# Gate and up products of an expert layer: two feed-forward tiles per accumulation group

## The chip, the cores and the metric

The kernel runs on one core of one Trainium2 chip. The metric is the device time of one execution in microseconds. Three executions of the kernel before gave 3181.3, 3182.09 and 3187.0 us, median 3182.09 us. One further execution was taken with the hardware profiler; every row below comes from it.

## What is computed

The program is one inference step of a two-layer backbone over 640 tokens (128 context, 512 latent) of width 1024. Layer 0 has a dense SwiGLU, layer 1 has eight SwiGLU experts of which each token takes two. Only the expert mixer is touched by the change:

```python
def swiglu(h, wg, wu, wd):
    return (jax.nn.silu(h @ wg) * (h @ wu)) @ wd       # 1024 -> 1408 -> 1024 for an expert

def moe_swiglu(h, router_w, router_b, wg, wu, wd):
    ...
    logits = (t @ router_w + router_b).astype(jnp.float32)
    top_v, top_i = lax.top_k(logits, TOP_K)             # 2 of 8
    w = jax.nn.softmax(top_v, axis=-1)
    gates = jnp.sum(jax.nn.one_hot(top_i, N_EXPERTS, dtype=jnp.float32) * w[..., None], axis=1).astype(t.dtype)
    y = jnp.zeros_like(t)
    for e in range(N_EXPERTS):
        y = y + gates[:, e:e + 1] * swiglu(t, wg[e], wu[e], wd[e])
    return y.reshape(B, L, D)
```

The reference computes it in float32. The kernel computes, of each expert, only the rows that chose it, and gets close to float32 with the rounded type fp32r: each operand is split into a high part (rounded to fp32r) and a low part (the operand minus its high part), and each product is the sum of three: high by high, high by low, low by high.

## The kernel before: the expert stage

**Items.** After routing, the rows of each expert lie in blocks of 128. There are `ITEMS` = 17 blocks, each with one expert's weights. An item needs 17 loads of weights (`ITEM_LOADS`): 11 of gate and up (`GU_LOADS` = `UF` = 11, the number of 128-wide tiles in 1408), and 6 of down (`DN_LOADS`), the last of which is half as long. A full load is 128 partitions by 2048 floats, 1 MB. A gate/up load holds, for one feed-forward tile f, all 8 blocks of the contraction (`KD` = 8), each with 128 gate columns and 128 up columns. q counts loads over all items, p within one item, i counts items.

**Slots.** A load lands in one of 8 slots (`M_SLOT`, `M_SLOTS`); its high part goes to one of 4 buffers (`M_HIGH`, `M_HI`); the low part overwrites the slot. SP's queue issues the even loads (L721), GpSimd's queue the odd ones (L2228); load q waits until TensorE has begun load q-7 (`m_used`, raised by a load's first matmul). SP's queue also carries an item's rows in (L726) and its results out (L730).

**TensorE** (L1259 to L1308), for each load of gate and up: wait for the low part of the load (`v_mlo`) and, at L1283, 24 matmuls (8 blocks by 3 products) of 256 moving columns into half of bank h % 2, h counting tiles over all items. Stationary are the rows, moving are the weights. After each tile but the first come the transposes of the tile before it (`turn_hidden`, L1267, one 128x128 transpose). After tile f = 8 (`M_TURN`) come the 8 transposes of the next item's rows (`turn_rows`, L1259). Then follow the down loads (L1305), 12 matmuls of 512 columns each; the transpose of the item's last tile is behind the first down load. Down load c reads the turned hidden tiles 2c and 2c+1.

**ScalarE**, at step p of an item: the high part of load q+3 (`moe_high`, L1581; it waits for the landing and for TensorE to have begun load q); at p = 0 the copies of the last item's results (`move_out`, L1596); silu of tile p's gate half (L1618, waits for TensorE, `s_mgu`); the high part of turned tile p-1 (L1589).

**VectorE**, at step p: the product silu by up of tile p (L1736, waits for silu); the low part of turned tile p-1 (L1740, waits for L1589); then the low part of load q+2 (`moe_low`, L1659, waits for its high part). All engines work strictly in the order of their programs, so the low part of load q+2 stands behind the product of tile p. During down loads there is no tile; the low part of the last turned tile is at L1748, that of the next item's rows at L1727.

Of the kernel before, what the change touches and what calls it, by code (L numbers as in the profile page):

```python
# [26 lines left out]
ALU = mybir.AluOpType  # L27
ACT = mybir.ActivationFunctionType
# [5 lines left out]
P = 128  # L34
D = 1024
KD = D // P
# [24 lines left out]
ALPHA = (2 * DEPTH) ** 0.25  # L61
LN_EPS, RMS_EPS = 1e-5, 1e-6
NEG = -1e30
# [19 lines left out]
RING_W = 2 * KD * P  # L83
# [99 lines left out]
def build(nc, x_in, cond_in, ada_bias_in, const_in, par_in, ln_in, ada_in, feat_in, tokm_in, out_in,  # L183
          unit_in, down_in, moe_gu_in, moe_down_in, zero_in, ctx_na_k, ctx_na_v, ctx_df_k, ctx_df_v, state_in, table_in,
          y_prompt, y_sample, new_na_k, new_na_v, new_df_k, new_df_v, new_state):
    with ExitStack() as ctx:
# [28 lines left out]
        def bank(b, lo=0, hi=BANK):  # L215
            return psum[:, b * BANK + lo:b * BANK + hi]
# [6 lines left out]
        ident, upper, lower, ones, blocks = (keep[:, i * P:(i + 1) * P] for i in range(5))  # L223
# [59 lines left out]
        def changing4(ap, d, m):  # L283
# [48 lines left out]
        HG = [m_hg[:, i * P:(i + 1) * P] for i in range(4)]  # L332

        HB = R12[:, (M_HI + M_SLOTS - RING) * RING_W:][:, 0:TILES * D].rearrange("p (t d) -> p t d", t=TILES)

# [62 lines left out]
        s_mtr = sem("moe_hidden_turned")  # L398
# [5 lines left out]
        a_msg = sem("act_moe_silu")  # L404
# [6 lines left out]
        v_mh = sem("vec_moe_hidden")  # L411
# [156 lines left out]

        def m_item(q):
            return q // ITEM_LOADS, q % ITEM_LOADS  # L570

        ALL_M = ITEMS * ITEM_LOADS

# [180 lines left out]
        def _(pe):  # L754
# [507 lines left out]
            def turn_hidden(i, f):  # L1262
                h = UF * i + f
                pe.wait_ge(v_mh, h + 1)
                if h >= 2:
                    pe.wait_ge(v_mhl, h - 1)
                pe.transpose(bank(2 + h % 2, 0, P), HG[h % 4], ident).then_inc(s_mtr, 1)  # L1267

            pe.wait_ge(a_hb, 2 * TILES)
            turn_rows(0)  # L1270
            for i in range(ITEMS):
                for f in range(UF):
                    h, q = UF * i + f, m_load(i, f)
                    pe.wait_ge(v_mlo, q + 1)
                    if f == 0:
                        pe.wait_ge(v_mxl, i + 1)
                    if h >= 2:
                        pe.wait_ge(v_mh, h - 1)
                    hi, lo = (r32(w).rearrange("p (k c) -> p k c", k=KD) for w in (M_HIGH[q % M_HI], M_SLOT[q % M_SLOTS]))
                    for k in range(KD):  # L1280
                        cols = slice(k * P, (k + 1) * P)
                        for m, (x, w) in enumerate(((XT_HI, hi), (XT_HI, lo), (XT_LO, hi))):
                            mm = pe.matmul(bank(h % 2, 0, 2 * P), r32(x[:, cols]), w[:, k, :],  # L1283
                                           start=(k == 0 and m == 0), stop=(k == KD - 1 and m == 2))
                            if q and k == 0 and m == 0:
                                mm.then_inc(m_used, 1)
                    mm.then_inc(s_mgu, 1)
                    if f:
                        turn_hidden(i, f - 1)
                    if f == M_TURN and i + 1 < ITEMS:  # L1290
                        turn_rows(i + 1)
                for c in range(DN_LOADS):
                    p = GU_LOADS + c
                    q = m_load(i, p)
                    pe.wait_ge(v_mlo, q + 1)
                    if c == 0 and i:
                        pe.wait_ge(a_mo, 2 * i)
                    hi, lo = (r32(w) for w in (M_HIGH[q % M_HI], M_SLOT[q % M_SLOTS]))
                    for j in range(m_words(p) // D):
                        f = 2 * c + j  # L1300
                        pe.wait_ge(v_mhl, UF * i + f + 1)
                        for g in range(2):
                            at = slice(j * D + g * BANK, j * D + (g + 1) * BANK)
                            for m, (x, w) in enumerate(((GT_HI, hi), (GT_HI, lo), (GT_LO, hi))):
                                mm = pe.matmul(bank(4 + g), r32(x[:, f, :]), w[:, at],  # L1305
                                               start=(f == 0 and m == 0), stop=(f == UF - 1 and m == 2))
                                if j == 0 and g == 0 and m == 0:
                                    mm.then_inc(m_used, 1)  # L1308
                            if f == UF - 1:
                                mm.then_inc(s_mdn, 1)  # L1310
                    if c == 0:
                        turn_hidden(i, UF - 1)

        @block.scalar
        def _(act):
# [271 lines left out]
            def hidden_turned_high(h):  # L1587
                act.wait_ge(s_mtr, h + 1)
                act.copy(r32(GT_HI[:, h % UF, :]), bank(2 + h % 2, 0, P)).then_inc(a_mhh, 1)  # L1589

            def move_out(i):
                if i >= 2:
# [13 lines left out]
            for i in range(ITEMS):  # L1606
                for p in range(ITEM_LOADS):
                    q = m_load(i, p)
                    if q + M_AHEAD < ALL_M:
                        moe_high(q + M_AHEAD)  # L1610
                    if p == 0 and i:
                        move_out(i - 1)
                    if p < UF:
                        h = UF * i + p
                        act.wait_ge(s_mgu, h + 1)
                        if h >= 4:
                            act.wait_ge(s_mtr, h - 3)
                        act.activation(HG[h % 4], bank(h % 2, 0, P), ACT.Silu).then_inc(a_msg, 1)  # L1618
                    if 1 <= p <= UF:
                        hidden_turned_high(UF * i + p - 1)  # L1620
# [22 lines left out]
        def _(v):  # L1643
# [79 lines left out]
            def moe_items():  # L1723

                def rows_low(i):
                    v.wait_ge(a_mxh, i + 1)
                    v.tensor_tensor(r32(XT_LO), psum[:, 6 * BANK:8 * BANK], high(XT_HI), ALU.subtract).then_inc(v_mxl, 1)  # L1727

                rows_low(0)
                for i in range(ITEMS):  # L1730
                    for p in range(ITEM_LOADS):
                        q = m_load(i, p)
                        if p < UF:
                            h = UF * i + p
                            v.wait_ge(a_msg, h + 1)
                            v.tensor_tensor(HG[h % 4], HG[h % 4], bank(h % 2, P, 2 * P), ALU.mult).then_inc(v_mh, 1)  # L1736
                        if 1 <= p < UF:
                            h = UF * i + p - 1
                            v.wait_ge(a_mhh, h + 1)
                            v.tensor_tensor(r32(GT_LO[:, h % UF, :]), bank(2 + h % 2, 0, P), high(GT_HI[:, h % UF, :]),  # L1740
                                            ALU.subtract).then_inc(v_mhl, 1)
                        n = q + 2
                        if n < ALL_M:
                            moe_low(n)
                        if p == UF:
                            h = UF * i + p - 1
                            v.wait_ge(a_mhh, h + 1)
                            v.tensor_tensor(r32(GT_LO[:, h % UF, :]), bank(2 + h % 2, 0, P), high(GT_HI[:, h % UF, :]),  # L1748
                                            ALU.subtract).then_inc(v_mhl, 1)
                        if p == UF + 2 and i + 1 < ITEMS:  # L1750
                            rows_low(i + 1)

# [570 lines left out]
def lay_out(x_prompt, x_sample, cache_na_k, cache_na_v, cache_df_k, cache_df_v, state_dn, c, c_ctx, ada_w, ada_b, w_in,  # L2323
# [53 lines left out]
    def expert_tiles(w):  # L2377
        return w[0].reshape(EXPERTS, KD, P, UF, 1, P).transpose(0, 3, 2, 1, 4, 5)

    a["moe_gu"] = np.concatenate([expert_tiles(moe_w_gate), expert_tiles(moe_w_up)], 4).reshape(EXPERTS, UF, P, KD * 2 * P)  # L2380
# [34 lines left out]
```

## Time and profile before

| | |
|---|---|
| median of three executions | 3182.09 us |
| span of the profiled execution, first to last instruction | 3180.0 us |
| TensorE busy | 2834.8 us, 89% |
| VectorE busy | 1780.5 us, 56% |
| ScalarE busy | 1319.6 us, 41% |
| L1283, gate and up, weights' high part moving | 3728 matmuls, 571.2 us |
| L1283, gate and up, weights' low part moving | 760 matmuls, 215.2 us |
| L1305, down, by its larger group | 940 matmuls, 252.0 us |
| L1283 in the chain that ended last | 15% of the span |
| L1305 in the chain that ended last | 8% of the span |

How to read it: an engine's busy time is the time in which one of its instructions was running. Matmuls overlap, each starting while the one before it drains, so that the mean duration of one (287 ns at L1283) is longer than the distance from one start to the next. That distance is read from the starts in the timeline. The granted TensorE clock stands as a share of full speed: 1.00 is 2.4 GHz, 0.50 is 1.2 GHz. It is 1.00 in the expert stage from the end of its first loads on. The first matmul of the stage starts at 2259.9 us and the last one at 3121.2 us; behind it lie the gathering of the rows and the closing norm.

### The profile page before, as it was taken

How to read it: one execution, taken by the hardware profiler on the slowest of the kernel's cores; microseconds unless marked ns; L12 is line 12 of the kernel's file. 1: busy time of each engine (PE TensorE's matmuls, PEld its weight loads, DVE VectorE, ACT ScalarE, POOL GpSimd, SP SyncE). 2: the span in 40 equal slices, each digit the busy share in tenths (PEclk: the TensorE clock that was granted, in tenths of full speed). 3: DMA queues.
4: the chain of work that ended last, by engine and by line, in shares of the span. 5: the costliest groups of instructions: out<-in, count | busy, mean ns of one | idle time of the engine just before them, and what ended most of it. 6: DMA issues, size and time to landing. Idle time of an engine off the chain costs nothing.

```text
span 3180.0 us, 51506 instructions
## 1 busy us (share of the span) xinstructions
PE 2834.8 (89%) x21524; PEld 2516.3 (79%) x21524; DVE 1780.5 (56%) x2706; ACT 1319.6 (41%) x1934; POOL 341.3 (11%) x335
## 2 busy tenths in 40 slices
PE   6998897997799999979988979978699999999992
PEld 5996776666799899769977756667699989899992
DVE  2244445666722222352534456676588888888886
ACT  2123222445222122131342224442477777777773
POOL 0002213000200000100012130011100000000002
PEclk9998997899999999979988978999899999999996
DMA  5233221000112221232122110003699999999993
GB/s 211 80 132 131 82 82 41 19 1 1 54 67 73 80 80 64 89 138 76 54 97 107 56 47 13 1 1 134 233 380 353 375 350 364 365 359 376 354 366 122
DMA packets 76517, 477.43 MB, mean 150 GB/s; under 512 B 10224, under 2 KB 13808, under 8 KB 26864
## 3 DMA queue, kind: packets, MB, share of 16 engines
q1 hardware_dynamic: 52672, 316.84, 26.6%
q0 software_dynamic: 23616, 157.30, 13.1%
q8 instruction: 173, 2.83, 0.4%
q14 instruction: 56, 0.46, 0.0%
HBM read 455.49 MB, written 27.53 MB: 152 GB/s over the span
## 4 chain that ended last, share of the span: by engine, by line
PE 76%; DVE 10%; ACT 5%; issue 4%; DMA 3%; POOL 1%; DVEq 0%; SPq 0%; ACTq 0%
PE psum L1283 15%; PE psum L1182 10%; PE psum L832 8%; PE psum L1305 8%; PE psum L1212 4%; PE psum L1143 4%; PE psum L858 3%; PE psum L1090 3%; DMA ring<-in_ada 2%; PE psum L956 2%; PE psum L1048 2%; PE psum L966 2%; ACT stage_rounded L1581 2%; PE psum L979 2%; PE psum L771 1%
## 5 line engine op out<-in xcount | busy, mean ns | idle before, releaser
L1283 PE MATMUL psum<-stage_rounded 128*128 128x256 f32 x3728 | 571.2, 287 | 11.1 <-DVE stage_rounded L1659 4.3
L1283 PEld LDWEIGHTS psum<-stage_rounded 128*128 128x128 f32 x3728 | 512.4, 191 | 28.3 <-DVE ring_rounded L1659 12.0
L1659 DVE TENSOR_TENSOR ring_rounded<-ring,stage_rounded 128x2048 fp32r<-128x2048 f32 (+1 forms) x145 | 319.4, 2217 | 2.4 <-ACT stage_rounded L1581 2.4
L1659 DVE TENSOR_TENSOR stage_rounded<-stage,stage_rounded 128x2048 fp32r<-128x2048 f32 (+1 forms) x144 | 318.1, 2224 | 0.0
L1581 ACT CAST stage_rounded<-ring 128x2048 fp32r<-128x2048 f32 (+1 forms) x145 | 269.4, 1864 | 44.8 <-PE psum L1305 28.7
L1581 ACT CAST stage_rounded<-stage 128x2048 fp32r<-128x2048 f32 (+1 forms) x144 | 268.7, 1870 | 44.2 <-PE psum L1305 28.4
L1305 PE MATMUL psum<-stage_rounded 128*128 128x512 f32 x940 | 252.0, 394 | 0.1
L1476 ACT ACTIVATE stage<-psum,arena 128x640 f32<-128x640 f32 (+1 forms) x180 | 126.4, 706 | 231.0 <-DVE arena L1984 231.0
L1283 PE MATMUL psum<-ring_rounded,stage_rounded 128*128 128x256 f32 x760 | 215.2, 283 | 0.0
L1305 PEld LDWEIGHTS psum<-stage_rounded 128*128 128x128 f32 x940 | 175.1, 188 | 43.0 <-DVE stage_rounded L1659 3.9
L1090 PEld LDWEIGHTS psum<-stage 128*128 128x128 f32 x1008 | 134.0, 203 | 68.2 <-issue 35.4
L1090 PE MATMUL psum<-stage 128*128 128x128 f32 x1008 | 153.1, 299 | 30.4 <-ACT stage L1483 16.9
L1182 PE MATMUL psum<-stage_rounded 128*128 128x320 f32 x704 | 161.8, 311 | 12.0 <-POOL ring_rounded L2309 12.0
L1551 ACT CAST stage_rounded<-ring 128x2048 fp32r<-128x2048 f32 (+2 forms) x38 | 64.0, 1685 | 239.8 <-PE psum L1182 130.9
L1984 DVE TENSOR_REDUCE arena<-psum 128x1 f32<-128x640 f32 (+1 forms) x180 | 123.1, 713 | 72.0 <-PE psum L1051 36.4
L1182 PE MATMUL psum<-input_rounded,stage_rounded 128*128 128x320 f32 x704 | 161.4, 310 | 0.0
L1182 PE MATMUL psum<-stage_rounded,ring_rounded 128*128 128x320 f32 x704 | 161.1, 310 | 0.0
L1283 PEld LDWEIGHTS psum<-ring_rounded,stage_rounded 128*128 128x128 f32 x760 | 145.8, 192 | 0.3
L1452 ACT COPY stage<-psum 128x512 f32<-128x512 f32 x100 | 58.5, 585 | 211.0 <-PE psum L966 211.0
L2146 DVE TENSOR_TENSOR stage<-stage,psum 128x640 f32<-128x640 f32 x22 | 18.1, 822 | 216.4 <-PE psum L1182 216.4
L2126 DVE TENSOR_TENSOR ring_rounded<-ring,stage_rounded 128x2048 fp32r<-128x2048 f32 (+2 forms) x36 | 71.9, 1996 | 115.7 <-ACT stage_rounded L1551 115.7
L1212 PE MATMUL psum<-stage_rounded 128*128 128x512 f32 x440 | 135.9, 389 | 0.0
(318 smaller groups left out, 5990.6 us busy)
## 6 DMA issues: line engine op xcount, KB each, us to landing
ring<-in_ada SPq DMA_DIRECT2D x48, 1024.0 KB, 5.0
ring<-in_moe_gu SPq DMA_DIRECT2D x48, 1024.0 KB, 7.0
ring<-in_moe_gu POOLq DMA_DIRECT2D x47, 1024.0 KB, 7.3
stage<-in_moe_gu SPq DMA_DIRECT2D x46, 1024.0 KB, 7.8
stage<-in_moe_gu POOLq DMA_DIRECT2D x46, 1024.0 KB, 7.9
ring<-in_unit SPq DMA_DIRECT2D x22, 1024.0 KB, 4.8
stage<-in_moe_down SPq DMA_DIRECT2D x22, 1024.0 KB, 7.6
stage<-in_moe_down POOLq DMA_DIRECT2D x22, 1024.0 KB, 7.8
```

Source lines behind the costliest of these rows:

```text
L832: mm = pe.matmul(bank(b + g, 0, HALF), w[:, i % 2, k, :], r32(x[:, k, g * HALF:(g + 1) * HALF]), start=(k == 0 and m == 0), stop=(k == KD ...
L858: mm = pe.matmul(bank(b, 0, 256 if c < TOKM_LOADS else P), r32(x[:, k, t * P:(t + 1) * P]), wk, start=(k == 0 and m == 0), stop=(k == KD - ...
L1090: mm = pe.matmul(bank(7, 256, 256 + P), probT[j % 2][:, s * P:(s + 1) * P], VT[:, s, v_at:v_at + P], start=(s == 0), stop=(s == n - 1))
L1143: mm = pe.matmul(bank(n % 4, 0, 256), r32(x[:, k, t * P:(t + 1) * P]), w[:, k, :], start=(k == 0 and m == 0), stop=(k == KD - 1 and m == 2))
L1182: mm = pe.matmul(bank(b + 2 * i + g, 0, HALF), w[:, i, k, :], r32(x[:, k, g * HALF:(g + 1) * HALF]), start=(k == 0 and n == 0), stop=(k == ...
L1212: mm = pe.matmul(bank(b), r32(x[:, f, cols]), w[:, j, :], start=(f == 0 and m == 0), stop=(f == UF - 1 and m == 2))
L1283: mm = pe.matmul(bank(h % 2, 0, 2 * P), r32(x[:, cols]), w[:, k, :], start=(k == 0 and m == 0), stop=(k == KD - 1 and m == 2))
L1305: mm = pe.matmul(bank(4 + g), r32(x[:, f, :]), w[:, at], start=(f == 0 and m == 0), stop=(f == UF - 1 and m == 2))
L1476: act.activation(dst, src, ACT.Exp, bias=nb[:, s:s + 1], accum_out=sm[:, s:s + 1]).then_inc(a_exp, 1)
L1581: act.copy(r32(M_HIGH[q % M_HI][:, 0:n]), M_SLOT[q % M_SLOTS][:, 0:n]).then_inc(a_mhi, 1)
L1659: v.tensor_tensor(r32(w), w, high(M_HIGH[q % M_HI][:, 0:n]), ALU.subtract).then_inc(v_mlo, 1)
L1984: v.tensor_reduce(nb[:, s:s + 1], src, AX.XY if t else AX.X, ALU.max, negate=True).then_inc(v_nb, 1)
```

## The change

Two feed-forward tiles share one accumulation group, and so one PSUM bank in its full width. Of the 11 tiles, 10 form five wide groups and the last stays alone (`GROUPS` = 6; `m_group(p)` gives a load's group and whether it is the group's last load, `m_width(g)` its width, 256 or 128 hidden columns).

- A wide group's weights are 2 MB as before, in two loads; but each now holds half of the contraction (4 blocks) for both tiles, 256 gate and 256 up columns, where it held all 8 blocks for one tile. The host lays the weights out so. Size, number, slots and order of the loads stay.
- A load of a wide group has 12 matmuls of 512 columns (4 blocks by 3 products), where it had 24 of 256. The group ends with its second load. The eleventh load is as before.
- silu, the product, and the high and low parts of the turned tiles are done once per group, 256 columns wide, at the step of the group's last load; in between they are absent. The transposes come in pairs behind the next group; those of the last group stay behind the first down load. The transposes of the next item's rows come after group 4 (load 9), where they came after load 8.
- There are two hidden buffers of 256 columns for four of 128. silu of group h waits for the transposes of group h-2.
- VectorE's low part of load q+2 stays at step p, as does ScalarE's high part of load q+3. So the low part of a group's first load is at a step without a product, and that of a group's second load stands behind the product and the low part of turned hidden tiles.

```diff
-M_TURN = UF - 3
+GROUPS = (UF + 1) // 2
+M_TURN = GROUPS - 2
@@ TensorE
-                pe.transpose(bank(2 + h % 2, 0, P), HG[h % 4], ident).then_inc(s_mtr, 1)
+                for j in range(m_width(g) // P):
+                    mm = pe.transpose(bank(2 + h % 2, j * P, (j + 1) * P), HG[h % 2][:, j * P:(j + 1) * P], ident)
+                mm.then_inc(s_mtr, 1)
...
-                for f in range(UF):
+                for p in range(GU_LOADS):
+                    (g, last), q = m_group(p), m_load(i, p)
+                    h, wide = GROUPS * i + g, 2 * m_width(g)
                     pe.wait_ge(v_mlo, q + 1)
...
-                    for k in range(KD):
+                    for j in range(n):
+                        k = first + j
                         cols = slice(k * P, (k + 1) * P)
                         for m, (x, w) in enumerate(((XT_HI, hi), (XT_HI, lo), (XT_LO, hi))):
-                            mm = pe.matmul(bank(h % 2, 0, 2 * P), r32(x[:, cols]), w[:, k, :],
+                            mm = pe.matmul(bank(h % 2, 0, wide), r32(x[:, cols]), w[:, j, :],
                                            start=(k == 0 and m == 0), stop=(k == KD - 1 and m == 2))
...
+                    if not last:
+                        continue
                     mm.then_inc(s_mgu, 1)
-                    if f:
-                        turn_hidden(i, f - 1)
-                    if f == M_TURN and i + 1 < ITEMS:
+                    if g:
+                        turn_hidden(i, g - 1)
+                    if g == M_TURN and i + 1 < ITEMS:
                         turn_rows(i + 1)
@@ ScalarE
-                    if p < UF:
-                        h = UF * i + p
+                    if p < UF and last:
+                        h, w = GROUPS * i + g, m_width(g)
                         act.wait_ge(s_mgu, h + 1)
-                        if h >= 4:
-                            act.wait_ge(s_mtr, h - 3)
-                        act.activation(HG[h % 4], bank(h % 2, 0, P), ACT.Silu).then_inc(a_msg, 1)
+                        if h >= 2:
+                            act.wait_ge(s_mtr, h - 1)
+                        act.activation(HG[h % 2][:, 0:w], bank(h % 2, 0, w), ACT.Silu).then_inc(a_msg, 1)
+                        if g:
+                            hidden_turned_high(i, g - 1)
@@ VectorE
-                        if p < UF:
-                            h = UF * i + p
+                        if p < UF and last:
                             v.wait_ge(a_msg, h + 1)
-                            v.tensor_tensor(HG[h % 4], HG[h % 4], bank(h % 2, P, 2 * P), ALU.mult).then_inc(v_mh, 1)
+                            v.tensor_tensor(HG[h % 2][:, 0:w], HG[h % 2][:, 0:w], bank(h % 2, w, 2 * w), ALU.mult).then_inc(v_mh, 1)
+                            if g:
+                                hidden_turned_low(i, g - 1)
                         n = q + 2
                         if n < ALL_M:
                             moe_low(n)
```

## Rows read from the trace of the kernel before

**Rows 1.** Busy time by window: us; PE, PEld, DVE, ACT, POOL, clock, DMA.
```profile
2400.00:2500.00 100.00, 98.92 (x694) 91.25 (x693) 84.18 (x81) 74.14 (x84) 8.97 (x17) 1.00 0.95 365
```

**Rows 2.** Chain of waits, 2440 to 2600 us: start us, us, what.
```profile
2469.87 3.13 PE psum L1283 x24
...
2473.11 2.87 PE psum L1283 x24
...
2491.78 0.87 PE psum L1259 x8
...
2520.53 3.13 PE psum L1283 x24
```

**Rows 3.** Timeline, one tile: start us, us, engine, line, operation, shapes, idle before.
```profile
2482.05 0.27 PE L1267 MATMUL psum<-arena,stage 128*128 128x128 f32 x1
...
2482.25 0.28 ACT L1618 ACTIVATE stage<-psum 128x128 f32<-128x128 f32 x1 [0.74 <-PE psum L1283]
...
2482.42 0.26 ACT L1589 CAST stage_rounded<-psum 128x128 fp32r<-128x128 f32 x1
...
2482.56 0.29 DVE L1736 TENSOR_TENSOR stage<-stage,psum 128x128 f32<-128x128 f32 x1 [0.30 <-ACT stage L1618]
...
2482.76 0.28 DVE L1740 TENSOR_TENSOR stage_rounded<-psum,stage_rounded 128x128 fp32r<-128x128 f32 x1
...
2482.96 2.28 DVE L1659 TENSOR_TENSOR ring_rounded<-ring,stage_rounded 128x2048 fp32r<-128x2048 f32 x1
...
2488.54 2.92 PEld L1283 LDWEIGHTS psum<-stage_rounded 128*128 128x128 f32 x24 [0.23 <-DVE stage_rounded L1659]
```

**Rows 4.** Timeline, first down load and what it waits for.
```profile
2498.35 0.27 PE L1267 MATMUL psum<-arena,stage 128*128 128x128 f32 x1
...
2498.61 2.61 PEld L1305 LDWEIGHTS psum<-stage_rounded 128*128 128x128 f32 x12 [0.23 <-DVE stage_rounded L1659]
...
2501.49 0.27 PE L1267 MATMUL psum<-arena,stage 128*128 128x128 f32 x1
2501.59 0.19 PEld L1305 LDWEIGHTS psum<-stage_rounded 128*128 128x128 f32 x1 [0.19 <-DVE ring_rounded L1659]
```

**Rows 5.** Timeline of TensorE, down loads in steady flow.
```profile
2508.98 0.61 PE L1305 MATMUL psum<-stage_rounded 128*128 128x512 f32 x2
...
2509.66 0.61 PE L1305 MATMUL psum<-stage_rounded 128*128 128x512 f32 x2
```

**Rows 6.** Groups by form: count, busy us, mean ns, idle before.
```profile
L1342 ACT COPY stage<-psum 128x256 f32<-128x256 f32 x48 | 17.7, 369 | 8.7 <-PE psum L771 8.7
...
L1423 ACT ACTIVATE stage<-psum 128x256 f32<-128x256 f32 x2 | 0.9, 432 | 0.0
L1423 ACT ACTIVATE arena<-psum 128x256 f32<-128x256 f32 x2 | 0.8, 394 | 0.0
...
L1736 DVE TENSOR_TENSOR stage<-stage,psum 128x128 f32<-128x128 f32 x187 | 53.8, 288 | 135.8 <-ACT stage L1618 135.8
L1928 DVE TENSOR_TENSOR stage<-stage,psum 128x256 f32<-128x256 f32 x120 | 50.6, 422 | 65.2 <-PE psum L979 50.0 <-PE psum L982 14.8
```

**Rows 7.** Timeline, start of an item on TensorE and ScalarE.
```profile
2513.09 1.92 ACT L1581 CAST stage_rounded<-stage 128x2048 fp32r<-128x2048 f32 x1 [0.80 <-PE psum L1305]
...
2516.70 1.08 ACT L1596 COPY stage<-psum 128x512 f32<-128x512 f32 x2
...
2513.97 5.92 PE L1283 MATMUL psum<-stage_rounded 128*128 128x256 f32 x48
2519.72 0.27 PE L1267 MATMUL psum<-arena,stage 128*128 128x128 f32 x1
```

**Rows 8.** The expert stage's transfers, median us to landing; ScalarE's waits for them.
```profile
stage<-in_moe_gu SPq DMA_DIRECT2D x46, 1024.0 KB, 7.8
...
L1581 ACT CAST stage_rounded<-stage 128x2048 fp32r<-128x2048 f32 x136 | 260.3, 1918 | 44.2 <-PE psum L1305 28.4 <-PE psum L1283 11.0 <-DMA stage<-in_moe_gu 1.1
```

**Rows 9.** Chain of waits, first loads of the stage, granted clock 0.50.
```profile
2259.91 7.25 PE psum L1283 x48
```

More of the change, by code:

```diff
@@ L331, in build @@
         OE = [m_out[:, i * D:(i + 1) * D] for i in range(2)]
-        HG = [m_hg[:, i * P:(i + 1) * P] for i in range(4)]
+        HG = [m_hg[:, i * 2 * P:(i + 1) * 2 * P] for i in range(2)]
         HB = R12[:, (M_HI + M_SLOTS - RING) * RING_W:][:, 0:TILES * D].rearrange("p (t d) -> p t d", t=TILES)
@@ L570, in m_item, with m_group, m_width @@
             return q // ITEM_LOADS, q % ITEM_LOADS
+        def m_group(p):
+            return p // 2, p % 2 == 1 or p == UF - 1
+        def m_width(g):
+            return 2 * P if g < GROUPS - 1 else P
         ALL_M = ITEMS * ITEM_LOADS
@@ L1311, in _ @@
                     if c == 0:
[L1312 removed]
+                        turn_hidden(i, GROUPS - 1)
         @block.scalar
@@ L1585, in rows_high, with hidden_turned_high @@
                 act.copy(r32(XT_HI), psum[:, 6 * BANK:8 * BANK]).then_inc(a_mxh, 1)
-            def hidden_turned_high(h):
+            def hidden_turned_high(i, g):
+                h, w = GROUPS * i + g, m_width(g)
                 act.wait_ge(s_mtr, h + 1)
-                act.copy(r32(GT_HI[:, h % UF, :]), bank(2 + h % 2, 0, P)).then_inc(a_mhh, 1)
+                act.copy(r32(GT_HI[:, 2 * g:2 * g + w // P, :]), bank(2 + h % 2, 0, w).rearrange("p (f t) -> p f t", t=P)).then_inc(a_mhh, 1)
             def move_out(i):
@@ L1612, in _ @@
                         move_out(i - 1)
[L1613 to L1614 removed]
+                    g, last = m_group(p)
+                    if p < UF and last:
+                        h, w = GROUPS * i + g, m_width(g)
                         act.wait_ge(s_mgu, h + 1)
[L1616 to L1620 removed]
+                        if h >= 2:
[3 more added lines that the diff above has]
+                            hidden_turned_high(i, g - 1)
+                    if p == UF:
+                        hidden_turned_high(i, GROUPS - 1)
                     if p == UF + 1 and i + 1 < ITEMS:
@@ L1727, in rows_low, with hidden_turned_low @@
                     v.tensor_tensor(r32(XT_LO), psum[:, 6 * BANK:8 * BANK], high(XT_HI), ALU.subtract).then_inc(v_mxl, 1)
+                def hidden_turned_low(i, g):
+                    h, w = GROUPS * i + g, m_width(g)
+                    v.wait_ge(a_mhh, h + 1)
+                    block = (slice(None), slice(2 * g, 2 * g + w // P), slice(None))
+                    v.tensor_tensor(r32(GT_LO[block]), bank(2 + h % 2, 0, w).rearrange("p (f t) -> p f t", t=P), high(GT_HI[block]),
+                                    ALU.subtract).then_inc(v_mhl, 1)
                 rows_low(0)
@@ L1732, in moe_items @@
                         q = m_load(i, p)
-                        if p < UF:
-                            h = UF * i + p
+                        g, last = m_group(p)
+                        if p < UF and last:
+                            h, w = GROUPS * i + g, m_width(g)
                             v.wait_ge(a_msg, h + 1)
-                            v.tensor_tensor(HG[h % 4], HG[h % 4], bank(h % 2, P, 2 * P), ALU.mult).then_inc(v_mh, 1)
[L1737 to L1741, printed above, removed]
+                            v.tensor_tensor(HG[h % 2][:, 0:w], HG[h % 2][:, 0:w], bank(h % 2, w, 2 * w), ALU.mult).then_inc(v_mh, 1)
+                            if g:
+                                hidden_turned_low(i, g - 1)
                         n = q + 2
@@ L1745, in moe_items @@
                         if p == UF:
[L1746 to L1749, printed above, removed]
+                            hidden_turned_low(i, GROUPS - 1)
                         if p == UF + 2 and i + 1 < ITEMS:
@@ L2375, in lay_out, with expert_tiles @@
     a["down"] = down.reshape(-1, UF, P, 2, BANK).transpose(0, 2, 3, 1, 4).reshape(-1, P, UF * D)
-    def expert_tiles(w):
-        return w[0].reshape(EXPERTS, KD, P, UF, 1, P).transpose(0, 3, 2, 1, 4, 5)
-    a["moe_gu"] = np.concatenate([expert_tiles(moe_w_gate), expert_tiles(moe_w_up)], 4).reshape(EXPERTS, UF, P, KD * 2 * P)
+    def expert_tiles(lo, n):
+        w = np.stack([m[0].reshape(EXPERTS, KD, P, UF, P)[:, :, :, lo:lo + n] for m in (moe_w_gate, moe_w_up)], 3)
+        return w.transpose(0, 2, 1, 3, 4, 5).reshape(EXPERTS, P, KD * 2 * n * P)
+    loads = [t for lo in range(0, UF - 1, 2) for t in np.split(expert_tiles(lo, 2), 2, -1)] + [expert_tiles(UF - 1, 1)]
+    a["moe_gu"] = np.stack(loads, 1)
     a["moe_down"] = moe_w_down[0].reshape(EXPERTS, UF, P, D).transpose(0, 2, 1, 3).reshape(EXPERTS, P, UF * D)
```

17 lines of the change are left out of this document (9 added, 8 removed).

## The prediction

> **What bounds the kernel now.** I read the windows first, then the chain of waits in the expert stage, then the timeline of one item. In a window of the stage TensorE is busy for 98.92 of 100 us at a clock of 1.00, VectorE for 84.18, ScalarE for 74.14, and the transfers' share is 0.95 at 365 GB/s [rows 1]. That looks like a stage that TensorE alone bounds, with two others close behind it. The chain repeats itself every 50.66 us (2469.87 to 2520.53), one item [rows 2]; 17 items are 861 us of the span. In it tiles of 2.87 us stand beside tiles of 3.13 us, though both are 24 matmuls of 256 columns [rows 2]. The longer ones began with a wait for VectorE: 0.23 us for L1659, the low part of the load [rows 3]. So the stage has a second bound that just touches the first. It is a chain across engines, and its steps can be read off for a narrow tile. TensorE ends it at 2482.05, where its next work, the transpose, begins; silu starts at 2482.25, the product at 2482.56, the low part of the turned tile at 2482.76 and the low part of the load at 2482.96, which lasts 2.28 us [rows 3]. That is 0.20 + 0.31 + 0.20 + 0.20 + 2.28 = 3.19 us, and 0.05 more to TensorE. The same 3.24 us lie between the end of an item's last tile at 2498.35 and the second down load, which waited until 2501.59 [rows 4]. TensorE has 2.87 us of matmuls and about 0.11 us for each transpose between two tiles' ends, two tiles for one such chain, so the chain costs it only 0.26 us at every other tile: 6.22 us for two tiles.
>
> **The wide matmul by itself.** In steady flow three down matmuls of 512 columns start in 2509.66 - 2508.98 = 0.68 us, 0.2267 us each [rows 5]; 24 matmuls of 256 columns take 2.87 us, 0.1196 each [rows 2]. A wide load is then 12 x 0.2267 = 2.72 us for 2.87, and ten of them save 1.5 us of TensorE's work per item, 25 us over 17 items. A load that begins after a wait costs more: the first down load took 2501.49 - 2498.61 = 2.88 us for its 12 matmuls [rows 4]. I take 2.88 for each wide load behind a wait and 2.72 for the others; the ends for both are 2.72 and 2.88. By the Trainium skill (TensorE: Matmul & The Clock Gate, Back-to-back issue gap) the distance of two matmuls is the columns over 2.4 GHz plus 2.5 ns, so two narrow ones at 109 ns each and one wide at 216 ns would be nearly equal in price, which speaks against any gain from width. The rows say otherwise, 239 against 227 ns; estimated by the page's figure, the six loads that count below would each be 0.13 us shorter, 13 us in all.
>
> **What the grouping does to the chain.** Call E the end of a wide group on TensorE. It turns the group before (0.22 us), then has the next group's first load ready, because its low part is now at a step without a product and was issued before VectorE began to wait. That load ends at E + 0.22 + 2.72 = E + 2.94. The second load's low part stands behind silu, product and turned low part of the group that ended at E, all 256 wide. VectorE's step from 128 to 256 columns out of PSUM is 422 - 288 = 0.134 us; ScalarE's silu has 280 ns at 128 columns, and at 256 columns its nearest rows have 369, 394 and 432 ns, so 0.09 to 0.15 us more; I take 0.11, from the row between [rows 3, 6]. The chain is 0.20 + 0.31 + 0.11 + 0.20 + 0.134 + 0.20 + 0.134 + 2.28 + 0.05 = 3.62 us. TensorE stands idle from 2.94 to 3.62, then needs 2.88: the next group ends at E + 6.50. Two tiles took 6.22. The idle time grows because work that was dealt out evenly, one product and one low part for each load, is now bunched in front of every second low part.
>
> **The sum for an item**, from the start of its first load:
> - loads 0 and 1, both ready: 2 x 2.72 = 5.44. Ready, since the high part of load 2 is done at 2513.09 + 1.92 and ScalarE's copies of results by 2517.78, before the group ends near 2519.4 [rows 7]. Before, this place lost 0.8 us, from 2519.72 to 2520.53, because tile 0's silu stood behind those copies [rows 2, 7].
> - group 1: no turned tile stands in the chain, so 3.62 - 0.334 = 3.29, and 2.88 behind it: 6.17.
> - groups 2, 3, 4: 3 x 6.50 = 19.50.
> - load 10, a narrow tile: two transposes 0.22, the next item's rows 0.87 [rows 2], and 2.87: 3.96, with no wait, as its low part follows at once on the one before it.
> - the second down load. Behind the narrow tile silu and product are short, and VectorE is free for the turned pair of group 4 at 0.20 + 0.31 + 0.20 = 0.71. Its high part is not there yet: ScalarE could start it at 0.37 if one transpose were enough, and with two between 0.37 and 0.48; I take 0.42, 0.37 us for the wide copy and 0.03 to VectorE (as from silu's end at 2482.53 to 2482.56 [rows 3]), 0.82. Then 0.334 + 2.28 + 0.05: 3.48.
> - from there the down loads are as before: 2513.97 - 2501.59 = 12.38 [rows 4, 7].
>
> The sum is 50.93 us against 50.66, 0.27 us more for an item, 17 x 0.27 = 4.6 us. TensorE's idle time rises to about 3.0 us an item: 0.57 at group 1, three times 0.68, 0.4 at the down loads.
>
> **What costs nothing, and by what cover.** The high parts on ScalarE (1.92 us each) start when TensorE has begun the load, so the one ahead of a silu is done about 0.7 us before the group ends; without that cover every 0.1 us is in the chain. The two hidden buffers are free in time: the transposes of group h-2 are a whole group old. SP's and GpSimd's queues are passed by nothing new; a transfer is issued when load q-7 begins and needed when load q-3 begins, four loads or 12 us later, and lands in 7.8 us; ScalarE waited 1.1 us in the whole stage for such landings in the slots' larger group [rows 8]. The number of transposes, bytes and instructions on the queues stays. The stage's first and last items have the same loads; I give them the same 0.27 us.
>
> The span would be 3180.0 + 4.6 = 3184.6 us, and the median stood 2.1 us over the profiled span: 3186.7 us.
>
> **Bounds of this case.** With 2.72 us behind a wait the item is 4 x 0.16 shorter, -11 us. With 2.88 for loads 0 and 1 too it is +5 us. silu at its ends moves four chains by -0.02 or +0.04 us, -1 or +3 us. So 3174 to 3195 us.
>
> **Rivals.**
> - *TensorE runs freely* (faster). If the chain did not hold the second loads, an item would be 10 x 2.72 + 2.87 for gate and up, 11 x 0.11 + 0.87 for transposes, 66 x 0.2267 = 14.96 for down: 47.1 us, 3.6 us less, and 61 us over all: 3121 us. For it: TensorE's 98.92% [rows 1]. Against it: the order on VectorE, and that the chain is seen already with less in it [rows 3, 4].
> - *ScalarE holds the chain, not VectorE* (slower). Behind a silu comes the high part of the turned tiles, 0.17 us after silu's start and 0.26 us long, and VectorE's low part followed it by 0.08 us at most [rows 3]. Widened by 0.11 each the copy ends at E + 0.85 and is seen at 0.88 (at 0.93 with the 0.08), where VectorE comes free at E + 0.955. Once it is seen later than that it decides, and each 0.1 us in groups 1 to 3 and 5 is 4 x 17 x 0.1 = 7 us. If both operations took twice their narrow time (0.56 and 0.52 us), the copy would be seen at 1.20, 0.245 us later than in my sum in three chains, 0.17 in group 0's (silu alone) and 0.15 in the last: 1.06 x 17 = 18 us, 3205 us; at a third of that, 3193 us. The rows of 256 columns stand against doubling [rows 6].
> - *The width gives nothing* (the change does not do what it says): a wide matmul takes 0.239 us, as two narrow ones. Six loads of 0.15 us more, 15 us: 3202 us. The down loads' pace speaks against it [rows 5].
> - *The clock falls.* TensorE idles after each group, and in the stage's first loads at a clock of 0.50 the 48 narrow matmuls took 7.25 us where 48 take 5.92 at 1.00 [rows 7, 9]. At 1.2 GHz a wide group is 24 x 0.453 + 0.44 = 11.3 us for 6.50; in half of the gate and up stretches that is some 12 us an item, 3390 us. Against it: 0.8 us of idle time at every item's start has left the clock at 1.00 [rows 1, 7]. The Trainium skill (TensorE: Matmul & The Clock Gate, A second HAM failure mode: psum-queue depth-cycling) tells of a kernel of 512-column matmuls whose short idles between groups made the clock oscillate; the window above shows short idles without that.
>
> **How the numbers follow.** My case 0.77, TensorE free 0.06, ScalarE's chain 0.10, no gain from width 0.05, the clock 0.02. The predicted time is 3186.7 us. The range goes from 3172 to 3200: my case with its bounds, and ScalarE's chain up to some two thirds of its price; it leaves out the free TensorE, the clock and the ends of the rest. About 0.2%, 6 us on either side of 3182.1, is what a measurement can tell here, so from 3176 to 3188 is no change. Of my case 0.04 is faster, 0.55 no change, 0.18 slower; with the rivals faster 0.10, same 0.55, slower 0.35.
>
> **What would show it.** The chain should repeat every 50.9 us. Loads 3, 5, 7 and 9 should begin with a wait for the low part of a load of about 0.6 to 0.7 us, the even ones with none, and the wait at the start of an item should go from 0.8 to 0.6 us, at load 3. TensorE's busy share of a window should fall from 98.9 to about 94%, and the starts of wide matmuls should be 0.227 us apart. From a group's end to the start of the low part on VectorE it should be 1.29 us. I am wrong if that distance is over 1.4 us or under 1.2, if odd loads start without a wait, or if the clock is below 1.00 behind the first loads.

## The result and the profile after

The changed kernel takes 3192.26 us (median of 15 executions, 3186.59 to 3197.71) where the kernel before takes 3186.75 us (15 executions, 3178.04 to 3190.41). The ratio is 1.002, with a 95% interval of 1.0012 to 1.0028: 4 to 9 us slower, about 6. The forecast was 4.6 us slower than before, and 3186.7 us as a time. That time is 5.6 us too low, and 4.7 us of this are the starting point: three executions of the kernel before had a median of 3182.09 us, fifteen have 3186.75. The forecast range, 3172 to 3200, holds the result.

In the profiled execution the span is 3190.5 us, 10.5 us longer than that of before. The first gate and up matmul starts at 2262.8 us (before: 2259.9) and the last down matmul at 3132.7 us (before: 3121.2). So 8.6 us are the expert stage's, 869.9 for 861.3 us; 2.9 us were lost ahead of it, in code that the change does not touch, and 1.0 us was won behind it. Such differences tell nothing: over the ten traces of this case the stage starts anywhere from 2259.9 to 2267.0 us.

Busy time by window, as in [rows 1]:

```profile
2400.00:2500.00 100.00, 95.81 (x443) 76.70 (x442) 82.65 (x58) 72.40 (x62) 8.83 (x17) 1.00 0.95 364
```

TensorE has fallen from 98.92 to 95.81 of 100 us at the same clock of 1.00. It needs less time for the same columns, and is idle for more.

The chain of waits through one item (start us, us, what), which answers to [rows 2]:

```profile
2477.84 3.07 PE psum L1297 x12
2480.93 0.39 ACT stage L1636
...
2481.35 0.42 DVE stage L1764
2481.77 0.34 DVE stage_rounded L1753
2482.10 2.21 DVE ring_rounded L1679
...
2484.36 3.03 PE psum L1297 x12
2487.41 0.39 ACT stage L1636
...
2501.51 2.89 PE psum L1297 x24
...
2507.72 12.58 PE psum L1321 x54
2520.30 5.45 PE psum L1297 x24
...
2528.87 3.07 PE psum L1297 x12
```

L1297 is the gate and up matmul, L1636 silu, L1764 the product, L1753 the turned low part, L1679 the low part of a load, L1321 the down matmul. In the chain of before every entry of the gate and up part was TensorE's, but for the one wait at an item's start. Now the chain leaves TensorE at each group's end, goes through silu, product, turned low part and the low part of a load, and comes back for one wide load of 12 matmuls. It repeats after 2528.87 - 2477.84 = 51.03 us.

The same stretch in the timeline, which answers to [rows 3, 4, 7]:

```profile
2469.10 8.32 PE L1297 MATMUL psum<-stage_rounded 128*128 128x512 f32 x36
2477.84 3.06 PE L1297 MATMUL psum<-stage_rounded 128*128 128x512 f32 x12 [0.41 <-DVE stage_rounded L1679]
2480.73 0.38 PE L1276 MATMUL psum<-arena,stage 128*128 128x128 f32 x2
...
2484.36 0.50 PE L1297 MATMUL psum<-stage_rounded 128*128 128x512 f32 x1 [0.47 <-DVE ring_rounded L1679]
...
2487.21 0.38 PE L1276 MATMUL psum<-arena,stage 128*128 128x128 f32 x2
```
```profile
2480.93 0.38 ACT L1636 ACTIVATE stage<-psum 128x256 f32<-128x256 f32 x1 [0.59 <-PE psum L1297]
2481.21 0.37 ACT L1606 CAST stage_rounded<-psum 128x256 fp32r<-128x256 f32 x1
```
```profile
2481.35 0.42 DVE L1764 TENSOR_TENSOR stage<-stage,psum 128x256 f32<-128x256 f32 x1 [1.36 <-ACT stage L1636]
2481.69 0.42 DVE L1753 TENSOR_TENSOR stage_rounded<-psum,stage_rounded 128x256 fp32r<-128x256 f32 x1
2482.02 4.48 DVE L1679 TENSOR_TENSOR ring_rounded<-ring,stage_rounded 128x2048 fp32r<-128x2048 f32 x2
```

From the group's end (2480.73, the first transpose) to silu 0.20 us, to the product 0.62, to the turned low part 0.96, to the low part of the load 1.29, and TensorE takes it up at 2484.36, 3.63 us after the group's end. The next group ends at 2487.21. VectorE's row of 4.48 us x2 shows the bunching: two low parts back to back, the second of which is early, the first late; and ahead of them VectorE stood idle for 1.36 us, waiting for silu.

### The profile page after: what moved, and what is told of

The parts are those of the page before. It is cut to its first block, busy times and chain, and to the rows that moved or that the text cites. A ratio compares the mean times of both kernels' runs of the same rounds, so it can differ in the third digit from the quotient of the medians.

```text
span 3190.5 us, 46833 instructions
## 1 busy us (share of the span) xinstructions
PE 2817.5 (88%) x19484; PEld 2401.4 (75%) x19484; DVE 1766.5 (55%) x2536; ACT 1302.3 (41%) x1764; POOL 341.5 (11%) x335
## 4 chain that ended last, share of the span: by engine, by line
PE 69%; DVE 16%; ACT 6%; issue 4%; DMA 4%; POOL 1%; SPq 0%; DVEq 0%; ACTq 0%; POOLq 0%
PE psum L1190 10%; PE psum L1297 9%; PE psum L840 8%; PE psum L1321 6%; PE psum L1220 4%; PE psum L1151 4%; PE psum L866 3%; DVE stage_rounded L1679 3%; DVE ring_rounded L1679 3%; PE psum L1098 3%; DMA ring<-in_ada 2%; PE psum L964 2%; PE psum L1056 2%; PE psum L974 2%; PE psum L987 1%
## 5 line engine op out<-in xcount | busy, mean ns | idle before, releaser
L1297 PE MATMUL psum<-stage_rounded 128*128 128x512 f32 (+1 forms) x2032 | 531.7, 381 | 36.1 <-DVE ring_rounded L1679 17.3
L1297 PEld LDWEIGHTS psum<-stage_rounded 128*128 128x128 f32 x2032 | 360.9, 189 | 129.5 <-DVE ring_rounded L1679 31.6
L1679 DVE TENSOR_TENSOR ring_rounded<-ring,stage_rounded 128x2048 fp32r<-128x2048 f32 (+1 forms) x145 | 317.4, 2218 | 2.8 <-ACT stage_rounded L1597 2.4
L1679 DVE TENSOR_TENSOR stage_rounded<-stage,stage_rounded 128x2048 fp32r<-128x2048 f32 (+1 forms) x144 | 316.1, 2224 | 0.5
L1321 PE MATMUL psum<-stage_rounded 128*128 128x512 f32 x940 | 252.4, 394 | 4.5 <-DVE stage_rounded L1679 2.2
L1321 PEld LDWEIGHTS psum<-stage_rounded 128*128 128x128 f32 x940 | 175.2, 188 | 46.5 <-DVE ring_rounded L1679 5.4
L1190 PE MATMUL psum<-stage_rounded 128*128 128x320 f32 x704 | 161.9, 311 | 12.0 <-POOL ring_rounded L2331 12.0
L1297 PE MATMUL psum<-ring_rounded,stage_rounded 128*128 128x512 f32 (+1 forms) x416 | 155.5, 374 | 0.0
L840 PE MATMUL psum<-stage_rounded 128*128 128x320 f32 x576 | 131.8, 309 | 3.0 <-DVE input L1791 3.0
```

The costliest lines, as they stand in the source:

```text
L840: mm = pe.matmul(bank(b + g, 0, HALF), w[:, i % 2, k, :], r32(x[:, k, g * HALF:(g + 1) * HALF]), start=(k == 0 and m == 0), stop=(k == KD ...
L1190: mm = pe.matmul(bank(b + 2 * i + g, 0, HALF), w[:, i, k, :], r32(x[:, k, g * HALF:(g + 1) * HALF]), start=(k == 0 and n == 0), stop=(k == ...
L1297: mm = pe.matmul(bank(h % 2, 0, wide), r32(x[:, cols]), w[:, j, :], start=(k == 0 and m == 0), stop=(k == KD - 1 and m == 2))
L1321: mm = pe.matmul(bank(4 + g), r32(x[:, f, :]), w[:, at], start=(f == 0 and m == 0), stop=(f == UF - 1 and m == 2))
L1679: v.tensor_tensor(r32(w), w, high(M_HIGH[q % M_HI][:, 0:n]), ALU.subtract).then_inc(v_mlo, 1)
```

## The experiments

All are compared with the kernel before in executions on the same chip. The theory: TensorE is held by one chain, in which the low part of a group's second load stands behind silu, product and turned low part; the wider matmul gives what its pace says, but only where TensorE is not waiting. The rivals: the transfers, ScalarE, no effect of width, a cost of the grouping itself.

**The order on VectorE undone.** In the changed kernel:

```diff
                         g, last = m_group(p)
+                        n = q + 2
+                        if n < ALL_M:
+                            moe_low(n)
                         if p < UF and last:
...
                             if g:
                                 hidden_turned_low(i, g - 1)
-                        n = q + 2
-                        if n < ALL_M:
-                            moe_low(n)
```

> The changed kernel; VectorE does the low part of load q+2 ahead of the product and of the turned low part in the same step, so no low part of a load stands behind silu. My theory: the 1.4 us for which TensorE is held at loads 3, 5, 7 and 9 and at the second down load comes only from that order. Then the chain is gone, TensorE runs freely, and an item takes 10 x 2.72 + 2.87 + 11 x 0.11 + 0.87 + 66 x 0.2267 = 47.1 us for the changed kernel's 51.03: 66 us less than the changed kernel, about 61 us less than before, ratio to before near 0.981. Rival, transfers: they were busy for 0.95 of the stage at 50.66 us an item, so if this share is their real limit an item can't be shorter than 48.1 us, ratio 0.986, and ScalarE's waits for landings grow from about 1 us to tens. Rival, ScalarE or something else holds the second loads: no gain, ratio 1.002.

Measured: 3131.18 us against 3183.68, ratio 0.9831 (0.9816 to 0.9846). The chain of waits of this run is TensorE's alone, and repeats after 2504.83 - 2457.48 = 47.35 us:

```profile
2457.48 10.88 PE psum L1297 x48
2468.36 0.22 PE psum L1276 x2
2468.58 5.50 PE psum L1297 x24
...
2492.54 12.29 PE psum L1321 x54
2504.83 10.88 PE psum L1297 x48
```
```profile
2500.00:2600.00 100.00, 100.00 (x483) 83.68 (x482) 89.11 (x63) 76.39 (x67) 9.54 (x18) 1.00 0.99 390
```

TensorE is busy for the whole 100 us. So it was the order on VectorE, and in an ordinary item nothing else that TensorE needed was late. The item is 0.25 us longer than the 47.1 of the sum: six wide loads behind transposes have 2.75 us where I put 2.72, and the down loads 15.03 for 14.96. The rival of a limit by transfers at 48.1 us an item is refuted: 390 GB/s were moved where 365 had looked like 0.95 of what there is. But its other sign came. From 2320 to 3080 us ScalarE waited 66.9 us for gate and up loads to land, where it waited 2.6 us in the kernel before. Two items took 49.3 and 48.7 us, and in the first of these the chain shows a late landing:

```profile
2700.05 16.81 DMA ring<-in_moe_gu
...
2716.89 1.92 ACT stage_rounded L1597
...
2718.83 2.30 DVE ring_rounded L1679
```

**The same order in the kernel before.**

```diff
+                        n = q + 2
+                        if n < ALL_M:
+                            moe_low(n)
                         if p < UF:
                             h = UF * i + p
...
-                        n = q + 2
-                        if n < ALL_M:
-                            moe_low(n)
```

> The kernel before with the same reordering on VectorE. My theory: its tiles lose 0.26 us at every other tile, 0.8 us at an item's start and some at the down loads to the same chain; without it an item takes 11 x 2.87 + 11 x 0.11 + 0.87 + 14.96 = 48.6 us for 50.66, 35 us less, ratio 0.989. The distance of this run to e1_changed_low_first is then what the wide matmuls give where nothing hides it: 1.5 us an item, 25 us. If width gives nothing of itself the two runs are equal.

Measured: 3150.8 us, ratio 0.990 (0.9883 to 0.9916), an item in 48.71 us, TensorE busy for 100.00 of 100 us. The chain was costing the kernel before 33 us as well. Between this run and the one above lie 3150.8 - 3131.18 = 20 us, and by the items 17 x (48.71 - 47.35) = 23 us: that is the change's gain where nothing hides it. I had expected 25.

**Width undone, grouping kept**, in the changed kernel and in its reordered form:

```diff
-                            mm = pe.matmul(bank(h % 2, 0, wide), r32(x[:, cols]), w[:, j, :],
-                                           start=(k == 0 and m == 0), stop=(k == KD - 1 and m == 2))
-                            if q and j == 0 and m == 0:
-                                mm.then_inc(m_used, 1)
+                            for at in range(0, wide, 2 * P):
+                                mm = pe.matmul(bank(h % 2, at, at + 2 * P), r32(x[:, cols]), w[:, j, at:at + 2 * P],
+                                               start=(k == 0 and m == 0 and at == 0), stop=(k == KD - 1 and m == 2 and at + 2 * P == wide))
+                                if q and j == 0 and m == 0 and at == 0:
+                                    mm.then_inc(m_used, 1)
```

> The changed kernel in all its grouping, but each matmul of 512 columns is two of 256 into the halves of the bank. Only width is undone. My theory: a load behind a wait takes about 3.03 us for 2.88 and a free one 2.87 for 2.72; the loads that end their group behind a wait (4) and loads 0 and 1 count, the others end in TensorE's idle time. 0.9 us an item, 15 us more than the changed kernel, ratio to before about 1.007. If width gives nothing: ratio stays 1.002. If width gave its whole 1.5 us an item even here, 25 us, 1.010.

Measured: 3201.34 us, ratio 1.0057 (1.0044 to 1.0071), an item in 51.67 us. Against the changed kernel's 51.03 that is 0.64 us an item, 11 us, where I had 0.9 and 15. The split load behind a wait is 3.16 us in the chain and the wide one 3.07, a difference of 0.09 where I had put 0.15; for the two free loads 5.77 and 5.45, 0.16 each, as expected. So width is worth 0.64 us an item in the changed kernel and 1.4 without the chain: the rest falls into TensorE's idle time. This run also splits the change in two: grouping alone takes an item from 50.67 to 51.67 us, 1.00 more, and width gives 0.64 back.

> e1_changed_low_first with each 512-column matmul split into two of 256: grouping without width, and no chain through VectorE. My theory: grouping by itself neither costs nor gives anything once the order on VectorE is right, so an item takes the 48.71 us that the kernel before took with its low parts first, ratio 0.990. If grouping has a cost of its own on TensorE (paired transposes, the bank's full width) the item is longer than 48.8 us; if it is what gave the gain of e1_changed_low_first over e2_before_low_first, the item stays near 47.35 us, ratio 0.983.

Measured: 3153.54 us, ratio 0.9906 (0.9887 to 0.9925), an item in 48.75 us, 0.04 more than the ungrouped kernel with the same order. With this order grouping by itself costs and gives nothing, so its 1.00 us of the run above is the chain's, and the whole gain of 1.4 us is the width's.

**A dose of the cause.** Only the turned low part moves behind the low part of the load, in the changed kernel, shown here, and in the kernel before:

```diff
                             v.tensor_tensor(HG[h % 2][:, 0:w], HG[h % 2][:, 0:w], bank(h % 2, w, 2 * w), ALU.mult).then_inc(v_mh, 1)
-                            if g:
-                                hidden_turned_low(i, g - 1)
                         n = q + 2
                         if n < ALL_M:
                             moe_low(n)
+                        if p < UF and last and g:
+                            hidden_turned_low(i, g - 1)
```

> The changed kernel; on VectorE only the turned low part (0.33 us) moves behind the low part of load q+2, the product stays ahead of it. A dose of the cause: if the chain through VectorE holds loads 5, 7 and 9, each group-to-group distance falls from 6.50 to 6.17 us, and the second down load no longer waits (0.45 us less). An item takes about 49.6 us for 51.03, 25 us less than the changed kernel, ratio to before 0.994. If ScalarE's copy of the turned tiles were what holds the chain, the low part of the load would be freed from it too and the gain would be larger than 0.33 us a group; if neither, nothing changes, ratio 1.002.

Measured: 3168.2 us, ratio 0.9946 (0.9933 to 0.996), an item in 49.50 us. The chain of waits, group to group:

```profile
2476.75 0.39 ACT stage L1636
2477.17 0.42 DVE stage L1764
2477.59 2.22 DVE ring_rounded L1679
2479.85 3.05 PE psum L1297 x12
2482.92 0.39 ACT stage L1636
```

2482.92 - 2476.75 = 6.17 us a group, the 6.17 of the expectation. The chain gave back just what was taken out of it. ScalarE's copy did not hold it: freed from it, the group would have become shorter still. The second down load, too, comes 0.45 us earlier, as expected: 3.05 us after the last tile's end for 3.50.

> The kernel before, on VectorE only the turned low part behind the low part of the load: the twin of e3_changed_turned_low_last. Its chain falls from 3.24 to 3.04 us; two tiles then need 3.04 + 2.87 = 5.91 us by the chain and 5.96 by TensorE's own work, so the waits at every other tile and at the down loads go, while the 0.8 us at an item's start stay. An item takes about 49.4 us for 50.66, 21 us less, ratio 0.993. If a small dose had no effect before (TensorE alone was the bound) the ratio is 1.000. If the ratio is 0.996 or more, the chain before was longer than I read it.

Measured: 3170.05 us, ratio 0.9958 (0.9943 to 0.9973), an item in 49.90 us. The gain is real but 0.76 us an item, not the 1.3 expected: three tiles of an item are still 2.94 us where 2.87 was free.

```profile
2480.11 2.94 PE psum L1283 x24
...
2483.16 2.87 PE psum L1283 x24
```

My expectation had left out that a load behind a wait costs 0.1 us more on TensorE. 3.04 + 2.97 = 6.01 us by the chain is over the 5.96 of TensorE's own work, and 2.94 + 0.11 + 2.87 + 0.11 = 6.03 were measured. The same correction fits the kernel before undisturbed: 3.24 + 2.98 = 6.22. Of the 0.5 us missing from the item's gain, 0.2 are these three tiles, 0.2 the second down load, which still waits, and 0.1 the free item itself, 48.71 us where I had put 48.6.

**The first item.** In the changed kernel it took 53.3 us, 2.2 more than the others. The trace shows two reasons:

```profile
2262.85:2266.00 3.15, 3.15 (x8) 2.50 (x9) 2.05 (x1) 0.39 (x1) 0.00 (x0) 0.52 0.02 5
```
```profile
2267.59 1.91 ACT L1597 CAST stage_rounded<-stage 128x2048 fp32r<-128x2048 f32 x1 [4.35 <-PE psum L1297]
2269.52 1.28 ACT L1636 ACT_TABLE_LOAD   x1
2270.81 0.38 ACT L1636 ACTIVATE stage<-psum 128x256 f32<-128x256 f32 x1
...
2273.91 0.50 PE L1297 MATMUL psum<-stage_rounded 128*128 128x512 f32 x1 [1.19 <-DVE ring_rounded L1679]
```

The granted clock is 0.50 for the first 3.05 us, and loads 0 and 1 take 7.00 us where they take 5.44 in the other items: 1.6 us. And silu's table is loaded at its first use. Before, this fell into ScalarE's wait for tile 0, since only one high part stood ahead; now two stand ahead, and the load is in the chain: load 3 begins 11.06 us after the item's start, 0.8 later than 8.73 and the 1.6 make. The next run loads the table earlier:

```diff
+            act.activation(misc[:, 718:719], ident[:, 0:1], ACT.Silu)
             rows_high(0)
```

> The changed kernel with one silu of a single column on ScalarE ahead of the first item's rows, so that the activation table is loaded while ScalarE waits for the rows anyway. In the changed kernel the table load of 1.28 us stands behind the high part of load 4 and in front of the first silu, in the chain. My theory: that is most of what the first item is longer than an undisturbed one; it falls from 53.4 us (first gate and up matmul to the first one of the next item) by 1.3 us, to 52.1. If it is the lower clock of its first load alone, the first item stays at 53.4. Outside the first item nothing changes; the time as a whole can't tell it, the trace can.

Measured, one execution of 3190.49 us: the first item took 52.5 us, 0.8 less, where I had expected 1.3.

```profile
2269.12 0.38 ACT L1637 ACTIVATE stage<-psum 128x256 f32<-128x256 f32 x1 [0.54 <-PE psum L1297]
...
2272.22 0.50 PE L1297 MATMUL psum<-stage_rounded 128*128 128x512 f32 x1 [0.41 <-DVE ring_rounded L1680]
```

Without the table load silu would have waited 0.54 us for TensorE anyway, so only some 0.75 of its 1.28 us were in the chain. Load 3 begins 10.26 us after the item's start, 0.80 earlier. The rest of the first item's excess is the clock: in the reordered run, where no chain holds TensorE, the first item still takes 1.6 us more than the others (48.99 for 47.35), with its first eight matmuls at the clock of 0.50.

The second item took 52.2 us in this run for 51.0 in the other, which is more than was gained:

```profile
2325.62 1.91 ACT L1597 CAST stage_rounded<-stage 128x2048 fp32r<-128x2048 f32 x1 [3.35 <-DMA stage<-in_moe_gu]
2327.43 0.37 ACT L1637 ACTIVATE stage<-psum 128x256 f32<-128x256 f32 x1
```

ScalarE stood at a load's landing and silu behind it came late. The two items together are 104.7 us with the early table and 104.2 without, so no gain in time is shown. The next run has a longer second item as well (48.6 us for 47.35); whether the early table load brings the late landing was not tried and stays open.

> e1_changed_low_first with the table load moved as in e6_changed_table_early: the fastest form that the runs so far point to. An item stays at 47.35 us, the first item may lose up to 1.3 us where the table load stood in the chain, and nothing where TensorE had both lows already. 3129 to 3131 us on a chip where before takes 3183, ratio 0.983. This run also repeats the former one with more rounds.

Measured: 3133.03 us, ratio 0.9834 (0.9818 to 0.9851). The first item was 48.94 us with it and 48.99 without: where no chain runs through ScalarE the table load is hidden. The form without it, 0.9831, is as good and simpler.

## Why the prediction was right, step by step

The steps of the item's sum against the timeline of the changed kernel (group ends at the first transpose):

| step | forecast us | measured us |
|---|---|---|
| loads 0 and 1 | 5.44 | 5.45 |
| group 1 | 6.17 | 6.18 |
| groups 2, 3, 4 | 6.50 each | 6.48, 6.52, 6.53 |
| load 10 with transposes | 3.96 | 3.96 |
| to the second down load | 3.48 | 3.50 |
| down loads | 12.38 | 12.42 |
| item | 50.93 | 51.03 |

- *The wide matmul by itself*: its free load at 2.72 us was right (5.45 for two), and so was 2.88 behind a wait: 2480.73 - 2477.84 = 2.89. That width gives 1.5 us where TensorE is free was shown by taking the chain away, 1.36 to 1.40 us.
- *The grouping and the chain*: forecast 3.62 us, measured 3.63. It comes out of the narrow rows plus 0.134 us for each wide VectorE operation and 0.11 for silu (it has 0.383 us in this trace, 0.10 more than the narrow one). The dose and the reordering show it as the cause.
- *The start of an item*: the wait at load 3 was forecast at 0.57 us and the narrow kernel's 0.8 us did go.
- *The second down load*: the step that the turned pair's high part is late was right, 3.50 for 3.48.
- *TensorE's share*: I had forecast 94% and the window has 95.81. The idle time by starts is near the forecast, 0.57 us at group 1 and 0.63 for 0.68 at groups 2 to 4 (the last matmul ahead of the wait starts at 2483.50 and has 0.227 us, the next one starts at 2484.36); but the view counts the modelled end of the last matmul as busy, so it shows 0.41 and 0.47 us of it. The forecast of a share should have been made in the terms of the view.
- *What costs nothing*: the copies and queues had the slack that I gave them, with one exception. I had set a landing of 7.8 us against a cover of 12 us, but 7.8 is a median. Of the gate and up loads issued from 2300 to 3040 us, 5 of 162 took over 12 us in the kernel before (longest 13.3), and 15 of 163 in the changed one (longest 14.5). ScalarE's waits for them rose from 1.1 to 11.3 us in the group that I had read, and from 1.5 to 18.7 us in the other. Most were hidden; in one item of 51.87 us this was not so:

```profile
2792.69 1.91 ACT L1597 CAST stage_rounded<-ring 128x2048 fp32r<-128x2048 f32 x1 [3.13 <-DMA ring<-in_moe_gu]
2794.50 0.37 ACT L1636 ACTIVATE stage<-psum 128x256 f32<-128x256 f32 x1
2797.92 0.50 PE L1297 MATMUL psum<-stage_rounded 128*128 128x512 f32 x1 [1.39 <-DVE ring_rounded L1679]
```

TensorE is idle for 1.39 us there, 0.9 more than at other groups. And the first item was not like the others, 1.9 us longer than before where I gave it 0.27.

Of the 8.6 us in the stage, sixteen items at 0.36 each make 5.8, the first item 1.9 and the late landing 0.9. The sum of the steps was thus off by 0.09 us an item, 1.4 us in all, and 2.5 us, the first item's excess and the landing, stood in no term of it. That the two medians lie 5.5 us apart, so near to the forecast 4.6, is in part luck; the interval of 4 to 9 us holds the trace's 8.6 as well.

- *The rivals*: TensorE free was the state of the first experiment, 47.35 us an item for the 47.1 forecast, and not that of the change. ScalarE's copy ended at 2481.21 + 0.37 = 2481.58, 0.11 us ahead of VectorE's low part at 2481.69, so it did not hold the chain. Width gave something, 0.64 us an item. The clock stayed at 1.00 with 0.47 us idle at every group.

Why the change did not pay: two loads take one pass of the chain and one load behind it, in the old form 3.24 + 2.98 = 6.22 us, in the new one 3.63 + 2.89 = 6.52. The width takes 0.09 us from the load, and three operations of double width put 0.39 into the chain, since they stand ahead of a low part that TensorE needs next and that does not depend on them. Changed and reordered, the kernel is 1.7% faster than before.

## What to carry to other kernels

When work units are made larger on one engine, look at what an in-order engine beside it has queued behind the completion of the larger unit: operations that do not depend on it, here the rounding of the next weights, must be ahead of it in program order. Two engines that just keep pace, seen as short waits at every second tile, mean that a saving on one is worth only a part until the chain between them is shortened (width 0.64 us an item here, for 1.4 without the chain); read that chain step by step from the timeline and redo the sum with the new widths. The same three-line reordering took the old form from 1 to 0.990 and the new one from 1.002 to 0.983, and only with it did the change gain anything. A median time to landing says nothing of the late ones: set the longest landings in the trace against the cover, not the middle one.

## What the runs showed of the hardware

- Matmuls of 256 columns start 0.120 us apart and those of 512 columns 0.227, at a clock of 1.00: 13 ns less for two narrow ones replaced by one wide. The Trainium skill (TensorE: Matmul & The Clock Gate, Back-to-back issue gap) would give 2.5 ns by its rule for isolated matmuls, and says itself that a stream with weight loads keeps another distance, about 131 ns for 512 columns. The trace agrees with neither, and the measured distance decides. The prediction used the rule for isolated matmuls alone.
- A load that begins after a wait costs TensorE 0.11 to 0.17 us more than its matmuls at their steady distance: 2.89 for 2.72 us when wide, 2.98 for 2.87 when narrow. Most of it lies between its first two matmuls: the wide one at 2484.36 us is followed 0.33 us later, where 0.227 is steady.
- Waits of 0.4 to 0.5 us after every wide group left the granted clock at 1.00 from 2266 us to the end of the stage.
- A transfer share of 0.95 at 365 GB/s was no limit: with faster engines the same transfers ran at 390 GB/s and 0.99. But the landings spread: 1 MB loads with a median of 7 to 8 us took up to 13.3 us in the kernel before, 14.5 in the changed one and 16.8 in the reordered one, where 5 of 162, 15 of 163 and 19 of 175 took over 12 us. Why single ones are late was not tried and stays open.
